# Moving the decayed-key products of a gated-recurrence mixer from GpSimd to VectorE

## The chip, the core and the metric

The kernel is one program on one NeuronCore of a Trainium2 chip. The core has five engines that run their own instruction streams and meet only at semaphores: TensorE (PE, matrix products and transposes; its weight loads are a row of their own, PEld), VectorE (DVE), ScalarE (ACT), GpSimd (POOL) and SyncE (SP, which here only issues DMAs). The metric is the device time of one execution in microseconds; the shown time is a median of several.

## What is computed

One inference step of a one-layer hybrid encoder over 1024 prompt rows and 32 sample rows of width 1024: a modulated norm, one input projection to 4096 columns, a retention mixer with 4 heads and an HGRN2 mixer with 4 heads, an output projection, a two-level mixture of experts, a last norm. The change touches the HGRN2 part:

```python
def hgrn2_chunk(S, q, k, v, logf):
    b = jnp.cumsum(logf, axis=1)
    inter = jnp.einsum('blhk,bhkv->blhv', q * jnp.exp(b), S)
    diff = b[:, :, None] - b[:, None, :]
    dec = jnp.exp(jnp.where(causal[None, :, :, None, None], diff, -jnp.inf))
    A = jnp.einsum('blhk,bmhk,blmhk->bhlm', q, k, dec)
    intra = jnp.einsum('bhlm,bmhv->blhv', A, v)
    k_dec = k * jnp.exp(bl[:, None] - b)          # bl is b at the chunk's last frame
    S_new = jnp.exp(bl)[..., None] * S + jnp.einsum('blhk,blhv->bhkv', k_dec, v)
```

Each head's output is then divided by its root mean square, scaled and gated.

## The kernel before

The program has five phases, one after the other: condition, mixers, output, experts, combine. Only `phase_mixers` is touched. It runs a hardware loop of 4 rounds, one pair of heads (one retention, one HGRN2) a round. A round first makes 12 transposed pieces of the projection on PE (`turned_piece`, lines 703 to 705), and then goes through 9 tiles of rows: tiles 0 to 7 of 128 rows, and tile 8, the sample's 32 rows. The tile loop is software-pipelined over 11 turns by hand: in turn i an engine works on tile i (projection, queries, keys, rotary), on tile i-1 (scores, masks, state products) and on tile i-2 (norm, output). Each engine's order is the order in which this code issues it; nothing else reorders it.

For one tile of the HGRN2 head these steps matter:

- `differences(i)`, DVE lines 885 to 894: a scan makes the running sum of the log decays in plane 8 of the tile `decay`, then plane 0 (distance to the tile's end) and planes 1 to 7 (distances to the middle of blocks of seven sizes, the levels).
- `decays(i)`, ACT lines 567 and 571: absolute value and exponential of all nine planes, in place; then `exp_done`.
- `queries(i)`, DVE lines 902 to 906: `last_f`, `q_in` = plane 8 times the queries (128 elements a partition), `q_lv` = planes 1 to 7 times the queries (896 elements).
- `keys(i)`, POOL line 495: `k_lv` = planes 0 to 7 times the keys `hk` (1024 elements); then `kl_done`.
- `rotary(i)`, DVE lines 987 to 994: rotates the retention head's query and key out of `qkv` and ends with `rot_done`.
- `values(i)`, ACT lines 641 and 644: copies `qkv` out of PSUM, waits for `rot_done`, makes the retention head's decayed key `k_dec`.
- `squares_of`, ACT lines 595 to 604: sums of squares of tile i-2 and a first estimate of its inverse root. `refine`, POOL lines 507 to 514: one Newton step on 128 x 2 numbers. `normalise`, ACT line 612: applies it.
- `copies`, ACT line 621: copies the three transposed tiles of tile i-1 out of PSUM (`turned`), which opens `scored(i-1)` on DVE, lines 964 to 977, then `gated`, lines 949 and 954.
- On PE: half a projection of tile i (12 matmuls, lines 729 to 731), in turns 1 to 8 eight small matmuls of the modulation (line 812), `scores(i-1)` (lines 744 to 766; it waits for `rot_done`, `kl_done`, `ql_done`), `turn_out(i-2)` (line 824; it waits for `normalise`), `retention_scores(i-1)` (line 775), the other half of the projection, `mix(i-1)` (lines 791 to 803).

ACT's order within a turn is fixed as: `squares_of(i-2)`, `normalise(i-2)`, `copies(i-1)`, `decays(i)`, `wide_levels(i-1)`, `values(i)`. DVE's is: `state(i-2)`, `differences(i)`, `scored(i-1)`, `gated(i-2)`, `queries(i)`, `rotary(i)`. POOL's is: `refine(i-2)`, `keys(i)`.

## Time and profile before

| | us |
|---|---|
| median of 3 runs | 1462.02 (1461.01 to 1463.92) |
| the profiled execution's own time | 1462.52 |
| its span, first to last instruction | 1460.9 |
| PE busy in the span | 1201.8 (82%) |
| DVE busy | 866.7 (59%) |
| ACT busy | 638.0 (44%) |
| POOL busy | 216.6 (15%) |
| POOL line 495 (`k_lv`), 40 instructions | 79.1 |

A busy share is an average over phases with different limits, so it does not say what bounds the mixers; the rows further down are read for that. "Idle before" and the name behind the arrow tell how long an engine had stood still before an instruction and which instruction ended the wait.

### The profile page before, as it was taken

Reading aid. Unit: us, or ns where it says so; the run is one execution under the profiler, and the core shown is the slowest. Engines: PE = TensorE matmul, PEld = TensorE weight load, DVE = VectorE, ACT = ScalarE, POOL = GpSimd, SP = SyncE. Lnnn points to the kernel's source line nnn. Section 1 sums busy time; section 2 is a strip of 40 time slices with the busy share of each in tenths; the row PEclk is TensorE's granted clock in tenths of the full one; section 3 lists DMA queues with packets and bytes.
Section 4 is the critical chain, followed back from the end, with each engine's and each line's share of the span. In section 5 each row is a group of like instructions: output and inputs, shape, how many; then the busy total and the mean of one; then the engine's idle time right before and its main releaser. Section 6 shows DMA issues by size and latency. Waiting matters only on the chain. (4 is left out here: it accounts for less than half of the span.)

```text
span 1460.9 us, 25004 instructions
## 1 busy us (share of the span) xinstructions
PE 1201.8 (82%) x7899; PEld 971.0 (66%) x7900; DVE 866.7 (59%) x1812; ACT 638.0 (44%) x1250; POOL 216.6 (15%) x307
## 2 busy tenths in 40 slices
PE   6479998999899989999489972989899999899900
PEld 1178776977597768877368751777677777777800
DVE  2614883368526872488545666677755575557339
ACT  3333554444434453345422213466544465446224
POOL 0200220022102220122000113011111101011132
PEclk9779999999999999999699985999899999999965
DMA  7512212221222122320453315979966696766155
GB/s 281 166 44 80 63 55 64 74 64 55 62 67 73 55 59 60 88 80 16 161 142 117 120 52 185 336 259 322 318 222 213 216 327 198 278 230 230 58 193 209
DMA packets 201385, 215.29 MB, mean 147 GB/s; under 512 B 15368, under 2 KB 166464, under 8 KB 201024
## 3 DMA queue, kind: packets, MB, share of 16 engines
q1 hardware_dynamic: 179136, 174.40, 37.6%
q0 software_dynamic: 10064, 34.42, 6.4%
q10 hardware_dynamic: 12112, 5.41, 1.3%
q8 instruction: 56, 0.92, 0.3%
q14 instruction: 17, 0.14, 0.0%
HBM read 187.40 MB, written 26.79 MB: 147 GB/s over the span
## 5 line engine op out<-in xcount | busy, mean ns | idle before, releaser
L703 PE MATMUL mixers_ps_proj<-early_h_hi,mixers_w_hi 128*128 128x352 f32 x384 | 127.7, 333 | 32.6 <-POOL mixers_a_hg L482 27.6
L1740 PE MATMUL experts_ps_g<-experts_w_hi,experts_x_hi 128*128 128x512 f32 x384 | 150.5, 392 | 2.2 <-DVE experts_x_lo L1669 2.2
L1742 PE MATMUL experts_ps_g<-experts_w_hi,experts_x_lo 128*128 128x512 f32 x384 | 150.2, 391 | 0.0
L1741 PE MATMUL experts_ps_g<-experts_w_lo,experts_x_hi 128*128 128x512 f32 x384 | 150.2, 391 | 0.0
L1664 DVE TENSOR_TENSOR experts_w_lo<-all_raw,experts_w_hi 128x1024 fp32r<-128x1024 f32 x96 | 113.9, 1223 | 28.3 <-ACT experts_w_hi L1613 25.2
L495 POOL TENSOR_TENSOR mixers_k_lv<-mixers_decay,mixers_hk 128x1024 f32<-128x1024 f32 (+2 forms) x40 | 79.1, 1981 | 334.4 <-ACT mixers_decay L571 334.4
L729 PE MATMUL mixers_ps_proj<-mixers_w_hi,early_h_hi 128*128 128x512 f32 (+1 forms) x288 | 119.1, 413 | 9.9 <-DVE mixers_w_lo L856 9.9
L704 PE MATMUL mixers_ps_proj<-early_h_lo,mixers_w_hi 128*128 128x352 f32 x384 | 125.8, 328 | 0.0
L705 PE MATMUL mixers_ps_proj<-early_h_hi,mixers_w_lo 128*128 128x352 f32 x384 | 125.8, 328 | 0.0
L1664 DVE TENSOR_TENSOR experts_w_lo<-experts_raw_more,experts_w_hi 128x1024 fp32r<-128x1024 f32 x96 | 111.8, 1222 | 14.5 <-ACT experts_w_hi L1613 13.1
L731 PE MATMUL mixers_ps_proj<-mixers_w_hi,early_h_lo 128*128 128x512 f32 (+1 forms) x288 | 113.7, 395 | 0.0
L730 PE MATMUL mixers_ps_proj<-mixers_w_lo,early_h_hi 128*128 128x512 f32 (+1 forms) x288 | 113.4, 394 | 0.0
L1613 ACT ACTIVATE experts_w_hi<-all_raw 128x1024 fp32r<-128x1024 f32 x96 | 97.7, 1055 | 13.6 <-PE experts_ps_g L1742 11.0
L856 DVE TENSOR_TENSOR mixers_w_lo<-all_raw,mixers_w_hi 128x1024 fp32r<-128x1024 f32 x32 | 43.3, 1366 | 93.7 <-ACT mixers_w_hi L529 93.7
L703 PEld LDWEIGHTS mixers_ps_proj<-early_h_hi,mixers_w_hi 128*128 128x128 f32 x384 | 74.5, 194 | 34.4 <-POOL mixers_a_hg L482 27.8
L1613 ACT ACTIVATE experts_w_hi<-experts_raw_more 128x1024 fp32r<-128x1024 f32 x96 | 94.4, 1059 | 0.0
L1740 PEld LDWEIGHTS experts_ps_g<-experts_w_hi,experts_x_hi 128*128 128x128 f32 x384 | 72.6, 189 | 17.6 <-issue 2.6
L1741 PEld LDWEIGHTS experts_ps_g<-experts_w_lo,experts_x_hi 128*128 128x128 f32 x384 | 72.7, 189 | 15.1
L1742 PEld LDWEIGHTS experts_ps_g<-experts_w_hi,experts_x_lo 128*128 128x128 f32 x384 | 72.6, 189 | 15.2
L1764 PE MATMUL experts_ps_y<-experts_w_hi,experts_h_hi 128*128 128x512 f32 x192 | 80.8, 421 | 0.3
L1765 PE MATMUL experts_ps_y<-experts_w_lo,experts_h_hi 128*128 128x512 f32 x192 | 78.0, 406 | 0.0
L1274 PE MATMUL output_ps_o<-output_w_hi,output_o_hi 128*128 128x512 f32 (+1 forms) x144 | 61.7, 428 | 19.8 <-DVE output_o_lo L1304 19.8
(269 smaller groups left out, 2613.9 us busy)
## 6 DMA issues: line engine op xcount, KB each, us to landing
experts_raw_more<-in_W_down_e_dram SPq DMA_DIRECT2D x128, 256.0 KB
all_raw<-in_W_gate_e_dram SPq DMA_DIRECT2D x96, 256.0 KB, 5.9
all_raw<-in_W_up_e_dram SPq DMA_DIRECT2D x96, 256.0 KB, 6.6
all_raw<-in_W_in_dram SPq DMA_DIRECT2D x32, 512.0 KB, 4.2
all_raw<-in_W_ada_dram SPq DMA_DIRECT2D x32, 512.0 KB, 3.9
y_scratch<-experts_y POOLq DMA_DIRECT2D x24, 512.0 KB
condition_w_ada_in<-in_W_ada_dram SPq DMA_DIRECT2D x4, 2048.0 KB, 8.1
experts_raw_more<-in_W_gate_e_dram SPq DMA_DIRECT2D x32, 256.0 KB
```

The source lines that it names most:

```text
L703: pe.matmul(out, whi, xhi, start=(k == 0), stop=False)
L704: pe.matmul(out, whi, xlo, start=False, stop=False)
L705: last = pe.matmul(out, wlo, xhi, start=False, stop=(k == KD - 1))
L729: pe.matmul(out, xhi, whi, start=(k == 0), stop=False)
L730: pe.matmul(out, xhi, wlo, start=False, stop=False)
L731: last = pe.matmul(out, xlo, whi, start=False, stop=(k == KD - 1))
L1613: act.activation(w_hi[:, c], raw[c], ACT.Copy).then_inc(hi_done, 1)
L1664: dve.tensor_tensor(w_lo[:, c], raw[c], f32(w_hi[:, c]), ALU.subtract).then_inc(lo_done, 1)
L1740: pe.matmul(out, x_hi[:, k, :], w_hi[:, c, at], start=(k == 0), stop=False)
L1741: pe.matmul(out, x_hi[:, k, :], w_lo[:, c, at], start=False, stop=False)
L1742: ins = pe.matmul(out, x_lo[:, k, :], w_hi[:, c, at], start=False, stop=(k == KD - 1))
L1764: pe.matmul(ps_y[m][:, :], h_hi[:, f, :], w_hi[:, 8 + f, at], start=(f == 0), stop=False)
```

## The change

The function `keys` leaves POOL's program and goes, with the same operands, into DVE's, between `queries(i)` and `rotary(i)`. Its waits for `exp_done` and `lv_done` are dropped there, because `queries(i)` has just waited for both on the same engine; the wait for `hk_done` in tile 0 stays. `refine` stays on POOL.

```diff
@@ -483,19 +483,6 @@
-                def keys(i):
-
-                    w = width(i)
-                    pool.wait_ge(exp_done, n[9] + (i + 1))
-                    pool.wait_ge(lv_done, n[9] + i)
-                    if i == 0:
-                        pool.wait_ge(hk_done, n[1] + 1)
-                    kb = hk[:, i * P:i * P + w]
-                    for c, (lo, hi) in enumerate([(0, 8)] if w == P else [(0, 1), (3, 8)]):
-                        last = pool.tensor_tensor(k_lv[:, lo:hi, 0:w], decay[:, lo:hi, 0:w],
-                                                  kb.unsqueeze(1).broadcast_to([P, hi - lo, w]), ALU.mult)
-                    last.then_inc(kl_done, 1)
@@ -516,8 +503,6 @@
                 for i in range(NT + 2):
                     if i >= 2:
                         refine(i - 2)
-                    if i < NT:
-                        keys(i)
@@ -907,6 +892,17 @@
+                def keys(i):
+
+                    w = width(i)
+                    if i == 0:
+                        dve.wait_ge(hk_done, n[1] + 1)
+                    kb = hk[:, i * P:i * P + w]
+                    for c, (lo, hi) in enumerate([(0, 8)] if w == P else [(0, 1), (3, 8)]):
+                        last = dve.tensor_tensor(k_lv[:, lo:hi, 0:w], decay[:, lo:hi, 0:w],
+                                                 kb.unsqueeze(1).broadcast_to([P, hi - lo, w]), ALU.mult)
+                    last.then_inc(kl_done, 1)
@@ -1005,6 +1001,7 @@
                     if i < NT:
                         queries(i)
+                        keys(i)
                         rotary(i)
```

DVE in turn 1, before, from the masks of tile 0 to the rotary step of tile 1:

```order
L973 TENSOR_REDUCE mixers_a_hg<-mixers_masked 32x32 x4
L977 ISA
L977 TENSOR_TENSOR mixers_a_ret<-mixers_ps_a,early_tables 128x128
L902 COPY mixers_last_f<-mixers_decay 128x1
L905 TENSOR_TENSOR mixers_q_in<-mixers_decay,mixers_hq 128x128
L906 TENSOR_TENSOR mixers_q_lv<-mixers_decay,mixers_hq 128x896
L987 TENSOR_TENSOR mixers_qk_cos<-mixers_qkv,early_tables 128x256
```

The same place after the change (later lines have moved up, by 15 before the new function and by 4 behind it):

```order
L969 TENSOR_REDUCE mixers_a_hg<-mixers_masked 32x32 x4
L973 ISA
L973 TENSOR_TENSOR mixers_a_ret<-mixers_ps_a,early_tables 128x128
L887 COPY mixers_last_f<-mixers_decay 128x1
L890 TENSOR_TENSOR mixers_q_in<-mixers_decay,mixers_hq 128x128
L891 TENSOR_TENSOR mixers_q_lv<-mixers_decay,mixers_hq 128x896
L902 TENSOR_TENSOR mixers_k_lv<-mixers_decay,mixers_hk 128x1024
L983 TENSOR_TENSOR mixers_qk_cos<-mixers_qkv,early_tables 128x256
```

One instruction of 1024 elements a partition now stands between `q_lv` and the rotary step; nothing else on DVE moved.

DVE in turn 8, where the tile has 32 columns, after the change:

```order
L890 TENSOR_TENSOR mixers_q_in<-mixers_decay,mixers_hq 128x32
L891 TENSOR_TENSOR mixers_q_lv<-mixers_decay,mixers_hq 128x5x32
L902 TENSOR_TENSOR mixers_k_lv<-mixers_decay,mixers_hk 128x32
L902 TENSOR_TENSOR mixers_k_lv<-mixers_decay,mixers_hk 128x5x32
L983 TENSOR_TENSOR mixers_qk_cos<-mixers_qkv,early_tables 32x256
```

Here two instructions stand in the new place.

POOL in one of the turns 2 to 7, before, the keys of one tile and then the refinement of an older one:

```order
L489 REGISTER_ALU
L495 TENSOR_TENSOR mixers_k_lv<-mixers_decay,mixers_hk 128x1024
L507 TENSOR_TENSOR mixers_norm<-mixers_norm 128x2
L508 REGISTER_ALU
L509 TENSOR_TENSOR mixers_norm<-mixers_norm,mixers_mean_sq 128x2
L510 REGISTER_ALU
L512 TENSOR_SCALAR mixers_norm<-mixers_norm 128x2
L513 REGISTER_ALU
L514 TENSOR_TENSOR mixers_norm<-mixers_norm 128x2
```

and after:

```order
L493 REGISTER_ALU
L494 TENSOR_TENSOR mixers_norm<-mixers_norm 128x2
L495 REGISTER_ALU
L496 TENSOR_TENSOR mixers_norm<-mixers_norm,mixers_mean_sq 128x2
L497 REGISTER_ALU
L499 TENSOR_SCALAR mixers_norm<-mixers_norm 128x2
L500 REGISTER_ALU
L501 TENSOR_TENSOR mixers_norm<-mixers_norm 128x2
```

POOL is left with the four small instructions of the refinement. PE, ACT and SP issue what they issued before.

## Rows read from the trace of the kernel before

**Rows 1.** The page's busy line; then who PE waited for, whole span.

```profile
PE 1201.8 (82%) x7899; PEld 971.0 (66%) x7900; DVE 866.7 (59%) x1812; ACT 638.0 (44%) x1250; POOL 216.6 (15%) x307
...
PE mixers_ps_ot L824 <- ACT mixers_normed L612: 28.4, 32, 2.8
```

**Rows 2.** Windows, round 2's tiles: length, PE, PEld, DVE, ACT, POOL, clock, DMA, GB/s.

```profile
448.00:557.00 109.00, 100.18 (x987) 75.86 (x988) 78.21 (x235) 50.79 (x153) 24.75 (x45) 0.97 0.22 64
```

**Rows 3.** Timeline of PE, round 2, turn 7 (start, duration, idle before).

```profile
527.24 0.41 PE L824 MATMUL mixers_ps_ot<-all_consts_sb,mixers_normed 128*128 128x128 f32 x2 [0.53 <-ACT mixers_normed L612]
```

**Rows 4.** Timeline of DVE, round 2, turn 6 and the start of turn 7.

```profile
516.23 0.29 DVE L964 TENSOR_TENSOR mixers_qd_t<-mixers_turned,early_tables 128x128 f32<-128x128 f32 x1 [1.66 <-ACT mixers_turned L621]
...
519.89 1.17 DVE L905 TENSOR_TENSOR mixers_q_in<-mixers_decay,mixers_hq 128x128 f32<-128x128 f32 x1
520.98 1.08 DVE L906 TENSOR_TENSOR mixers_q_lv<-mixers_decay,mixers_hq 128x896 f32<-128x896 f32 x1
521.98 0.41 DVE L987 TENSOR_TENSOR mixers_qk_cos<-mixers_qkv,early_tables 128x256 f32<-128x256 f32 x1
...
522.97 0.29 DVE L994 TENSOR_TENSOR mixers_rot<-mixers_qk_cos,mixers_qk_sin 128x128 f32<-128x128 f32 x1
...
527.51 0.29 DVE L964 TENSOR_TENSOR mixers_qd_t<-mixers_turned,early_tables 128x128 f32<-128x128 f32 x1 [1.66 <-ACT mixers_turned L621]
```

**Rows 5.** Timeline of ACT, the same stretch.

```profile
523.29 0.40 ACT L644 ACTIVATE mixers_k_dec<-mixers_rot,mixers_kd_col 128x128 f32<-128x128 f32 x1 [3.14 <-DVE mixers_rot L994]
...
523.85 0.28 ACT L595 ACTIVATE mixers_squares<-mixers_ps_o 128x128 f32<-128x128 f32 x1 [0.15 <-issue]
...
526.47 0.63 ACT L612 ACTIVATE mixers_normed<-mixers_ps_o,mixers_norm 128x128 f32<-128x128 f32 x2 [1.24 <-POOL mixers_norm L514]
526.99 0.49 ACT L621 ACTIVATE mixers_turned<-mixers_ps_tr 128x384 f32<-128x384 f32 x1
```

**Rows 6.** Timeline of POOL, the same stretch.

```profile
518.53 2.37 POOL L495 TENSOR_TENSOR mixers_k_lv<-mixers_decay,mixers_hk 128x1024 f32<-128x1024 f32 x1 [3.38 <-ACT mixers_decay L571]
525.30 0.19 POOL L507 TENSOR_TENSOR mixers_norm<-mixers_norm 128x2 f32<-128x2 f32 x1 [4.40 <-ACT mixers_mean_sq L604]
...
526.24 0.20 POOL L514 TENSOR_TENSOR mixers_norm<-mixers_norm 128x2 f32<-128x2 f32 x1
```

**Rows 7.** Timeline of DVE, round 2, end of the pieces and turn 0.

```profile
446.72 1.23 DVE L856 TENSOR_TENSOR mixers_w_lo<-all_raw,mixers_w_hi 128x1024 fp32r<-128x1024 f32 x1 [0.42 <-ACT mixers_w_hi L529]
...
447.92 0.28 DVE L905 TENSOR_TENSOR mixers_q_in<-mixers_decay,mixers_hq 128x128 f32<-128x128 f32 x1
448.12 1.08 DVE L906 TENSOR_TENSOR mixers_q_lv<-mixers_decay,mixers_hq 128x896 f32<-128x896 f32 x1
454.57 0.43 DVE L987 TENSOR_TENSOR mixers_qk_cos<-mixers_qkv,early_tables 128x256 f32<-128x256 f32 x1 [5.36 <-ACT mixers_qkv L641]
```

**Rows 8.** DVE groups by shape, 97 to 700 us (busy, mean ns).

```profile
L905 DVE TENSOR_TENSOR mixers_q_in<-mixers_decay,mixers_hq 128x128 f32<-128x128 f32 x32 | 36.0, 1125 | 0.0
```

**Rows 9.** Timeline of DVE, round 2, turn 1.

```profile
462.64 1.74 DVE L905 TENSOR_TENSOR mixers_q_in<-mixers_decay,mixers_hq 128x128 f32<-128x128 f32 x1
464.31 1.08 DVE L906 TENSOR_TENSOR mixers_q_lv<-mixers_decay,mixers_hq 128x896 f32<-128x896 f32 x1
```

**Rows 10.** Timeline of DVE, round 2, turn 8.

```profile
542.43 0.17 DVE L905 TENSOR_TENSOR mixers_q_in<-mixers_decay,mixers_hq 128x32 f32<-128x32 f32 x1
542.53 0.31 DVE L906 TENSOR_TENSOR mixers_q_lv<-mixers_decay,mixers_hq 128x160 f32<-128x160 f32 x1
542.77 0.41 DVE L987 TENSOR_TENSOR mixers_qk_cos<-mixers_qkv,early_tables 32x256 f32<-32x256 f32 x1
```

**Rows 11.** Timeline of PE, round 2, turn 9, scores of tile 8.

```profile
544.17 0.28 PE L744 MATMUL mixers_ps_tr<-all_consts_sb,mixers_rot 32*128 32x32 f32 x2 [0.71 <-DVE mixers_rot L994]
```

**Rows 12.** Timeline of POOL, round 2, turn 4, first step of a refinement.

```profile
491.28 0.38 POOL L507 TENSOR_TENSOR mixers_norm<-mixers_norm 128x2 f32<-128x2 f32 x1 [4.41 <-ACT mixers_mean_sq L604]
```

**Rows 13.** Windows, round 2, turn 9, columns as in rows 2.

```profile
549.00:553.00 4.00, 3.46 (x13) 1.74 (x13) 2.04 (x6) 0.05 (x1) 0.00 (x0) 0.50 0.30 82
```

## The prediction

> **What bounds the kernel now.** The page gives PE as the busiest engine by far, 1201.8 of 1460.9 us, DVE 866.7, POOL 216.6 [rows 1]. In the stretch of round 2 that holds the tile turns PE is busy 100.2 of 109 us and DVE 78.2 [rows 2]. By shares the change looks harmless or good: the engine with the most room to wait gives work to one that has 31 us free. The next view says otherwise. The list of PE's waits shows one that comes back in each turn: the transposes of `turn_out` (line 824) wait for ACT's normalised tile (line 612), 32 times, 28.4 us in all [rows 1]; in a middle turn it is 0.53 us [rows 3]. So in each turn something other than PE ends last, and the third view, the timelines of one turn on DVE, ACT and POOL, is read backwards from there. Start to start:
>
> DVE 516.23 (masks, `scored`) to 519.89 (`q_in`), 3.66; to 520.98 (`q_lv`), 1.09; to 521.98 (rotary), 1.00; to 522.97 (its last step), 0.99 [rows 4]. ACT's `k_dec` starts 0.32 later, at 523.29, after 3.14 us of waiting for just that step; its squares at 523.85 (0.56) [rows 5]. POOL's refinement starts at 525.30 (1.45) and its last step at 526.24 (0.94) [rows 6]. ACT normalises at 526.47 (0.23) and copies `turned` at 526.99 (0.52) [rows 5]. DVE's next `scored` starts at 527.51 (0.52), after 1.66 us of waiting for that copy [rows 4]. The sum is 11.28 us, and that is the turn's length (527.51 less 516.23). This is a closed ring: **DVE's stretch from `scored` to rotary lies in it**, since ACT cannot begin the squares before `k_dec`, which waits for rotary. PE's work of a turn is 0.53 us shorter than the ring. Whatever is added to DVE between the masks and the last step of rotary lengthens each turn in full.
>
> POOL's key product is not in the ring: it starts at 518.53, runs 2.37 and ends at 520.90 [rows 6], and PE asks for it only behind rotary and the half projection. But it costs the ring something all the same. `q_in` has 128 elements and takes 0.28 us in turn 0, where POOL is idle [rows 7], and 1.17 in turn 6 [rows 4]: it starts at 519.89 and is done at 521.06, just behind POOL's end at 520.90. In turn 1 it takes 1.74 [rows 9]. I read it as blocked until POOL has finished.
>
> The Trainium skill says the same: in "SBUF — State Buffer", section "SBUF: two separate sides", VectorE and GpSimd share one port pair as an exclusive lock, held for a whole instruction, when VectorE reads two SBUF inputs. By that rule the excess of `q_in` must vanish with the key product; the trace agrees (0.28 against 1.17). The figures for it in the sum are those of the rows.
>
> **The change, part by part.**
>
> *Taken off DVE: the blocked time of `q_in`.* Its 32 wide instances hold 36.0 us [rows 8]. Four are turn 0 at 0.28 [rows 7] and four are turn 1 at 1.74 [rows 9]; that leaves 27.9 us for the 24 of turns 2 to 7, 1.163 each. The next instruction starts 0.08 before the end (1.17 long, 1.09 to the next start) [rows 4]. So it occupies 1.083 of the ring, and 0.20 once free (447.92 to 448.12) [rows 7]: **0.883 saved** in each of 24 turns. In turn 1 it is 464.31 less 462.64, 1.67 [rows 9], so 1.47 is saved there, 4 times.
>
> *Put on DVE: the key product.* No row shows it on DVE. The nearest is `q_lv`, the same operation and types over 896 elements: 1.08 us, 1.00 to the next start [rows 4]. 128 elements take 0.28, so 768 more take 0.80, or 1.04 ns each, and 1024 elements take 1.08 + 0.13 = 1.21. A two-input subtraction of 1024 elements takes 1.23 [rows 7]. Less the overlap of 0.08 this is **1.14 added** to the ring. Bounds: 1.00 (as `q_lv`) and 1.23 (no overlap).
>
> *Turns 2 to 7:* 1.14 - 0.883 = +0.257; 24 of them give **+6.2 us**. The saving is smaller than the price because the blocked time was only the tail of POOL's 2.37 us; its first 1.36 (518.53 to 519.89) lay beside DVE's masks and output products.
>
> *Turn 1:* 1.14 - 1.47 = -0.33, four times, **-1.3 us**. PE's 32 waits at line 824 are eight a round, and the first of the eight stands behind turn 1 [rows 1], so PE follows.
>
> *Turn 8:* the 32-column tile. `q_in` takes 0.17, so it was not blocked; the two new instructions cost 0.10 (as `q_in`'s 542.43 to 542.53) and 0.24 (as `q_lv`'s 542.53 to 542.77) [rows 10]. PE waits for this rotary directly, 0.71 us [rows 11], and nothing covers it: 4 x 0.34 = **+1.4 us**.
>
> *Turn 0:* the key product lands behind `q_lv` (448.12), ahead of 5.36 us in which DVE waits for the first projection [rows 7]: nothing; without that cover it would be 1.14, four times. Its absence from POOL frees the second last weight split on DVE, but the last one, at 446.72, waits for ACT anyway (0.42 idle) [rows 7]: nothing.
>
> *Who now gets its keys later.* Before they were there at 520.90; after at about 519.89 + 0.20 + 1.00 + 1.21 = 522.30. PE's scores want them together with the last step of rotary, which starts at 522.97 [rows 4] and will start later, so no new wait. `differences` waits for `kl_done`, now its own engine's and long given. POOL loses its wait for the exponentials, and the refinement stands first in its queue; it was started by ACT's squares before, with POOL 4.40 us idle [rows 6], so this gives nothing.
>
> *A term with no fixed sign.* The first step of the refinement takes 0.19 us [rows 6] or 0.38 [rows 12], in the same place, beside DVE's `differences`. It is in the ring. Of the 24 in turns 3 to 8, 7 are longer than 0.19 and 17 are not, and a shift of some 0.01 us in the start seems to decide. After the change all could be short, 7 x -0.19 = -1.3 us, or all long, 17 x 0.19 = +3.2. I take no change.
>
> Sum: 6.2 - 1.3 + 1.4 = **+6.2 us** (rounded only here). Phases before and behind the mixers hold none of these steps and start one after the other, so the span goes from 1460.9 to 1467.1, the profiled run from 1462.5 to 1468.7, and the median, 0.5 below it, to **1468.2 us**.
>
> **Rivals.**
>
> *The turn is not held by the ring (no change).* If ACT or POOL had slack that I do not see, for instance if the squares could start on something other than `k_dec`, the 0.257 would be absorbed, and with it turn 1's gain; only turn 8 would stay: 0 to +1.4, so 1462.0 to 1463.4. For it: DVE has 1.66 us free in a turn. Against it: that idle time is a wait for the ring's own last link, and the ring's links sum to the turn without a remainder. Chance 0.08. The key product priced at 1.00 with all refinements short (+6.2 less 28 x 0.14 less 1.3, about +1.0) also ends here: 0.04.
>
> *POOL's key product was the slow thing (faster).* If the scores or the squares did wait for the keys in some way that the releasers hide, giving them to the engine that makes them in 1.21 instead of 2.37 would shorten turns 1 to 7 by up to 1.16 less the 0.257 that DVE adds, 28 x 0.9 = 25 us: 1437. It decides if the keys are the last of the scores' inputs; the rows have them ready 2.1 us ahead of rotary's last step (520.90 against 522.97) [rows 4, 6]. Half of such an effect would do for a visible gain. Chance 0.05. The Trainium skill supports the move as such: "GPSIMD Engine Reference", section "Engine selection", puts elementwise products of two inputs on VectorE because GpSimd is about half as fast. The trace shows that ratio (2.37 against an estimated 1.21), but the rule compares durations and says nothing of what lies beside other work.
>
> *`q_in` is not blocked by POOL (much slower).* If its 1.17 us came from something else in that place, such as reading the exponentials just written, nothing would be saved: 28 x 1.14 + 1.4 = +33, so 1495. It decides if `q_in` stays above 1 us. Against it: 0.28 in turn 0 and 0.17 in turn 8, and the end that follows POOL's in turn 6. Chance 0.03.
>
> *TensorE loses its clock more often (slower).* The granted clock is 0.97 over the turns [rows 2], and it falls to 0.50, the 1.2 GHz level, in turn 9, where PE has stood still for longer [rows 13]. If the longer waits brought such a stretch of 4 us at half speed or more into turns 1 to 8 of a round, PE would lose some 2 us or more each time: +8 or more on top, about 1476. Against it: PE waited 28.4/32 = 0.89 us a turn on average at that clock [rows 1], and would now wait some 0.2 more. Chance 0.03.
>
> *All refinements long:* +9.4, 1471.4. Chance 0.04.
>
> **How the numbers follow.** The forecast has the rest, 0.73. Slower by over 0.2% (2.9 us, about what a measurement of this kernel can tell from no change): 0.73 + 0.03 + 0.03 + 0.04 = 0.83. Within: 0.12. Faster: 0.05. The ends: the key product at 1.00 instead of 1.14 takes 3.9 us off, which with short refinements gives 1463.0; at 1.23 it adds 2.5, with long ones 1473.9. Both terms at their ends at once is unlikely, so the range takes the middle of them and the edge of the next cases: 1464.3 to 1472.2.
>
> **What would show it.** `q_in` at 0.28 in all wide turns; the key product on DVE at 1.21, the next start 1.14 behind it; turns of 11.53 us in place of 11.28, turn 1 shorter by 0.33; PE's wait at line 824 up from 0.53 to about 0.8; POOL with only its four small steps; POOL's 79 us of key products gone and DVE busier by some 10 us in all (32 x 1.21 and 4 x 0.48 on, 27 us of blocked `q_in` and some of the weight splits off). The forecast is wrong if turns keep 11.28 (the ring is not what I think), if `q_in` stays long, or if the clock in turns 1 to 8 falls below what it was.

## The result, and the profile after

| | before | changed |
|---|---|---|
| median, beside each other on one chip | 1461.51 (4 runs, 1460.63 to 1463.92) | 1470.97 (4 runs, 1470.53 to 1478.55) |
| ratio, with its 95% interval | | 1.0079 [1.0052, 1.0106] |
| profiled execution; its span | 1462.52; 1460.9 | 1478.55; 1476.7 |

The changed kernel is slower, by 7.6 to 15.5 us. The forecast was slower by 6.2 (a ratio of 1.0042): the sign is right, the size too small. Two further runs of the changed kernel took 1474.59 and 1475.13. A repeat of the pair gave 1.011 [1.0079, 1.014]. So the profile has to answer two questions: are the steps of the forecast there at their sizes, and where is the rest?

The page of the changed kernel (busy line) and the list of PE's waits, which answer [rows 1]:

```profile
PE 1208.2 (82%) x7899; PEld 975.7 (66%) x7900; DVE 872.2 (59%) x1852; ACT 637.6 (43%) x1250; POOL 138.5 (9%) x267
...
PE mixers_ps_ot L809 <- ACT mixers_normed L597: 32.8, 32, 2.9
...
PE mixers_ps_proj L688 <- ACT mixers_hk L540: 5.1, 3, 1.9
PE mixers_ps_tr L729 <- DVE mixers_rot L990: 4.2, 4, 1.0
```

POOL loses 78.1 us. PE's wait for the normalised tile grows by 4.4 us in all. The wait for `hk` is new: before, PE never waited for it. The wait for rotary's last step, in turn 9 of each round, was 2.8 us in all before and is 4.2 now.

Timeline of DVE, changed kernel, round 2, turn 6, which answers [rows 4]:

```profile
525.67 0.29 DVE L960 TENSOR_TENSOR mixers_qd_t<-mixers_turned,early_tables 128x128 f32<-128x128 f32 x1 [1.66 <-ACT mixers_turned L606]
...
529.33 0.27 DVE L890 TENSOR_TENSOR mixers_q_in<-mixers_decay,mixers_hq 128x128 f32<-128x128 f32 x1
529.53 1.07 DVE L891 TENSOR_TENSOR mixers_q_lv<-mixers_decay,mixers_hq 128x896 f32<-128x896 f32 x1
530.53 1.21 DVE L902 TENSOR_TENSOR mixers_k_lv<-mixers_decay,mixers_hk 128x1024 f32<-128x1024 f32 x1
531.67 0.41 DVE L983 TENSOR_TENSOR mixers_qk_cos<-mixers_qkv,early_tables 128x256 f32<-128x256 f32 x1
...
532.65 0.28 DVE L990 TENSOR_TENSOR mixers_rot<-mixers_qk_cos,mixers_qk_sin 128x128 f32<-128x128 f32 x1
...
537.19 0.29 DVE L960 TENSOR_TENSOR mixers_qd_t<-mixers_turned,early_tables 128x128 f32<-128x128 f32 x1 [1.66 <-ACT mixers_turned L606]
```

ACT, POOL and PE in the same turn, one after the other, which answer [rows 5], [rows 6] and [rows 3]:

```profile
532.97 0.40 ACT L629 ACTIVATE mixers_k_dec<-mixers_rot,mixers_kd_col 128x128 f32<-128x128 f32 x1 [3.35 <-DVE mixers_rot L990]
533.53 0.28 ACT L580 ACTIVATE mixers_squares<-mixers_ps_o 128x128 f32<-128x128 f32 x1 [0.16 <-issue]
...
536.15 0.63 ACT L597 ACTIVATE mixers_normed<-mixers_ps_o,mixers_norm 128x128 f32<-128x128 f32 x2 [1.25 <-POOL mixers_norm L501]
536.67 0.49 ACT L606 ACTIVATE mixers_turned<-mixers_ps_tr 128x384 f32<-128x384 f32 x1
```

```profile
534.98 0.20 POOL L494 TENSOR_TENSOR mixers_norm<-mixers_norm 128x2 f32<-128x2 f32 x1 [10.38 <-ACT mixers_mean_sq L589]
```

```profile
536.92 0.30 PE L809 MATMUL mixers_ps_ot<-all_consts_sb,mixers_normed 128*128 128x128 f32 x1 [0.76 <-ACT mixers_normed L597]
```

Read the ring again, start to start: 3.66 to `q_in`, 0.20, 1.00, 1.14 (the key product), 0.98 to rotary's last step, 0.32 to `k_dec`, 0.56, 1.45, 1.17, 0.52, 0.52. The sum is 11.52 us, against 11.28 before, and no link but the two edited ones moved by more than 0.01. The same view of turn 1 and the DVE groups by shape (97 to 715 us) answer [rows 8, 9]:

```profile
471.44 0.28 DVE L890 TENSOR_TENSOR mixers_q_in<-mixers_decay,mixers_hq 128x128 f32<-128x128 f32 x1
...
482.85 0.27 DVE L890 TENSOR_TENSOR mixers_q_in<-mixers_decay,mixers_hq 128x128 f32<-128x128 f32 x1
```

```profile
L902 DVE TENSOR_TENSOR mixers_k_lv<-mixers_decay,mixers_hk 128x1024 f32<-128x1024 f32 x32 | 38.7, 1208 | 0.0
...
L890 DVE TENSOR_TENSOR mixers_q_in<-mixers_decay,mixers_hq 128x128 f32<-128x128 f32 x32 | 8.7, 272 | 0.0
```

So the forecast's steps are there. For the rest the trace is cut at marks that both kernels have: the start of `q_in` in turns 0, 1 and 8 ("t0", "t1", "t8") and PE's `turn_out` of tiles 7 and 8 ("ot7", "ot8"), worked out from the timelines. Sums over the rounds:

```
us                                     before   changed   difference
start to the first projection piece     82.60     83.81      +1.2
first piece to t0 of round 0            50.94     51.29      +0.4
t0 to t1, 4 rounds                      58.91     60.24      +1.3
t1 to t8, 4 rounds                     319.09    323.33      +4.2
t8 to ot7, 4 rounds                     22.26     23.64      +1.4
ot7 to ot8, 4 rounds                    39.08     42.22      +3.1
ot8 to t0 of the next round, 3         140.08    142.31      +2.2
ot8 of round 3 to the output phase      10.84     11.42      +0.6
mixers: first piece to output phase    641.2     654.5      +13.3
```

The forecast's parts are the lines "t1 to t8" and "t8 to ot7": +5.6. Another 7.6 us of the mixers lies at the ends and starts of the rounds, where the change adds nothing. The remaining 2.5 us of the span lie outside the mixers, where executions of identical code also differ (from its first to its last product on PE, the experts' phase took 485.9 us before, 488.1 changed, and 478 to 502 in the traces of the kernels below, none of which touches it). The gap repeats in a second pair of traces, 639.9 and 653.2 us for the mixers; there the forecast's two lines give +6.6 and the rest +6.7.

What happens at a round's end shows in the windows (length, PE, PEld, DVE, ACT, POOL, granted clock, DMA, GB/s). Before, round 2's end, the stretches behind [rows 13]:

```profile
553.00:557.00 4.00, 4.00 (x18) 4.00 (x19) 0.61 (x2) 2.72 (x10) 0.73 (x4) 0.67 0.39 115
557.00:561.00 4.00, 2.41 (x16) 2.09 (x15) 1.62 (x4) 0.13 (x1) 0.00 (x0) 1.00 0.14 32
```

The changed kernel, the same place:

```profile
557.00:561.00 4.00, 2.11 (x9) 0.94 (x9) 2.57 (x8) 1.82 (x5) 0.37 (x2) 0.56 0.00 0
561.00:565.00 4.00, 4.00 (x14) 3.01 (x15) 0.90 (x3) 1.29 (x7) 0.21 (x2) 0.50 0.68 196
565.00:569.00 4.00, 4.00 (x19) 4.00 (x18) 0.00 (x0) 1.55 (x3) 0.53 (x3) 0.66 0.02 4
```

The clock is at its 1.2 GHz level (0.50) for 10.24 us at the end of rounds 0 to 2, where it was 6.82 before (548.80 to 555.62; now 557.48 to 567.72), and returns closer to the end of the next round's first piece. PE has no wait in that piece, so until the clock returns each matmul in it costs 0.29 us instead of 0.16. PE, before and then changed, around the point where the clock returns:

```profile
555.42 0.42 PE L705 MATMUL mixers_ps_proj<-early_h_hi,mixers_w_lo 128*128 128x352 f32 x1
555.68 0.32 PE L703 MATMUL mixers_ps_proj<-early_h_hi,mixers_w_hi 128*128 128x352 f32 x1
...
558.18 0.31 PE L824 MATMUL mixers_ps_ot<-all_consts_sb,mixers_normed 32*128 32x32 f32 x2
```

```profile
567.44 0.46 PE L690 MATMUL mixers_ps_proj<-early_h_hi,mixers_w_lo 128*128 128x352 f32 x1
567.74 0.32 PE L688 MATMUL mixers_ps_proj<-early_h_hi,mixers_w_hi 128*128 128x352 f32 x1
...
569.27 0.31 PE L809 MATMUL mixers_ps_ot<-all_consts_sb,mixers_normed 32*128 32x32 f32 x2
```

Before, 2.50 us of the piece ran at full speed ahead of `turn_out`; now 1.53.

The length of a low stretch by itself does not set the cost; where it ends does. Before, it ended 7.62 us behind ot7 in this round, and ot7 to ot8 took 10.18 us; in the changed kernel it ended 9.46 behind ot7, and the stretch took 11.01. In rounds 0 and 1 of the changed kernel the end lies 10.38 and 10.57 behind ot7, for 11.43 and 11.51 us. The same line runs through rounds 0 to 2 of all 14 traces of this study without a fill in turn 9 (12 kernels): 42 points, with 0.46 us more from ot7 to ot8 for each us that the low stretch ends later, and none more than 0.06 us off the line. From the matmuls one expects about that: in 1 us at 0.29 us each PE does 0.55 us of the work at 0.16.

A second thing follows on ACT's queue, which issues the store of the sample's state. Before, then changed, then PE in the changed kernel:

```profile
559.67 0.42 ACTq L651 DMA_DIRECT2D ut_state_ret_sample_dram<-mixers_s_sample  x1
...
561.51 1.28 ACT L554 ACT_TABLE_LOAD   x1 [4.38 <-issue]
```

```profile
570.76 1.72 ACTq L636 DMA_DIRECT2D ut_state_ret_sample_dram<-mixers_s_sample  x1
...
573.90 1.28 ACT L539 ACT_TABLE_LOAD   x1 [6.51 <-issue]
```

```profile
576.07 0.43 PE L688 MATMUL mixers_ps_proj<-early_h_hi,mixers_w_hi 128*128 128x352 f32 x1 [1.72 <-ACT mixers_hk L540]
```

The issue takes 0.42 us in every round before and 1.33, 1.05 and 1.72 in rounds 0 to 2 now. The sigmoids of the new round stand behind it on ACT and start later, and PE waits for `hk`: 3 times, 5.1 us. Its waits called "issue" at the same line shrank from 4.9 to 1.3, so 1.5 us of this is a net loss. Third, turn 0 of round 2 has a low stretch of its own that the kernel before has in no round. Windows over its start, before and then changed:

```profile
448.00:452.00 4.00, 3.93 (x17) 3.21 (x18) 1.21 (x3) 0.00 (x0) 0.00 (x0) 1.00 0.84 240
```

```profile
455.00:459.00 4.00, 3.51 (x9) 2.85 (x10) 2.76 (x5) 0.00 (x0) 0.00 (x0) 0.57 0.69 204
```

It begins (455.08) in PE's wait of 2.5 us for the last weight split, which both kernels have in every round, and turn 0 takes 16.09 us instead of 14.72.

### The profile page after: what moved, and what is told of

Read it like the earlier page. It is cut to its first block and busy times, and to the rows that moved or that the text cites. A ratio compares the mean times of both kernels' runs of the same rounds, so it can differ in the third digit from the quotient of the medians.

```text
span 1476.7 us, 24964 instructions
## 1 busy us (share of the span) xinstructions
PE 1208.2 (82%) x7899; PEld 975.7 (66%) x7900; DVE 872.2 (59%) x1852; ACT 637.6 (43%) x1250; POOL 138.5 (9%) x267
## 5 line engine op out<-in xcount | busy, mean ns | idle before, releaser
L841 DVE TENSOR_TENSOR mixers_w_lo<-all_raw,mixers_w_hi 128x1024 fp32r<-128x1024 f32 x32 | 38.6, 1221 | 98.5 <-ACT mixers_w_hi L514 98.5
L1720 PE MATMUL experts_ps_x<-all_consts_sb,experts_x_rows 128*128 128x128 f32 x200 | 32.4, 314 | 59.1 <-DMA experts_x_rows<-h_scratch,experts_index 59.1
```

## The experiments

Theory: the ring sets turns 1 to 7, and the surplus at the rounds' ends is a second cost. The rival for the first part is that the moved product hurts in some other way (contention on DVE, its effect on PE's scores). For the second part one theory is that the surplus comes from the product itself or from tile 8's small instructions, through PE's longer standstill in turns 8 and 9. The other is that any shift of a round's end can bring it (called the place theory).

**The pair again.** No edits: `a_again` is the changed kernel, `b_again` the one before.

> The changed kernel once more, unchanged, for a second trace and a tighter ratio. Ring theory (what the prediction rests on): turns 2 to 7 are 11.53 us in place of 11.28, in all some +6 us, so about 1468. Clock theory (a second cost beside the ring): TensorE's granted clock stays at 0.50 longer at the end of each round, 10.2 us against 6.8 in the profiled execution, and the sum is +9 to +12, about 1471 to 1474, with executions some us apart according to where the low stretches fall. A trace with 6.8 us at the end of the rounds and a time near 1468 would say that the profiled execution was an outlier.

> The kernel before once more, for a second trace. Clock theory: the low stretches at the end of the rounds have the same length in the three rounds, since the round's length (157.0 us) repeats; they may be 6.8 or 10.2 us. If they are 6.8 here too, the longer ones belong to the change and not to chance.

Measured: 1479.55 (1476.83 to 1480.98) beside 1462.47 (1453.36 to 1471.21), ratio 1.011; `b_again` 1462.27 in one run. The changed kernel came out above what either theory had asked for, while `b_again` agrees with the first run of before. The mixers take 653.2 and 639.9 us. In the changed kernel the low stretches at the ends are 10.24 us long again, the one in turn 0 of round 2 is there again, and long issues (0.84 to 1.21 us) are in it alone. `b_again` did not do as expected in one respect: its low stretches are 6.8, 6.8 and 10.2 us long, not of one length. The long one began 1.97 us ahead of ot7 and ended 8.27 behind it, and ot7 to ot8 took 10.47 us, not 11. Two traces of each kernel agree, so the extra cost belongs to the kernel, not to one execution.

**The ring.** `keys_last` puts the key product behind rotary, out of the ring:

```diff
                         queries(i)
-                        keys(i)
                         rotary(i)
+                        keys(i)
```

> Keys on VectorE as in the change, but behind the rotary step. Ring theory: q_in is free of GpSimd (-0.88 a turn) and the key product lies outside the ring, so the ring is 10.40 us and TensorE's own work of 10.75 takes over: turns of about 10.75 to 10.8, TensorE's wait for the normalised tile gone or under 0.1 us in turns 2 to 8; 24 to 28 turns x 0.5 = 12 to 14 us faster than before, about 1449. If the ring is not what sets the turn, it stays at 1462 or above.

Measured: 1450.68 (7 runs), ratio 0.9908 [0.987, 0.9946]. Turns of 10.78 us in the middle of a round, 10.70 in the mean of turns 1 to 7. Two of PE's waits:

```profile
PE mixers_ps_ot L809 <- ACT mixers_normed L597: 9.6, 4, 2.4
PE mixers_ps_tr L729 <- DVE mixers_k_lv L902: 4.7, 4, 1.2
```

Four waits for the normalised tile are left of 32, those of turn 9. The same instruction on the same engine, some 1.2 us later in the order, costs nothing in turns 2 to 8. In turn 9 the scores now wait for the small tile's key products, 4.7 us in all, where they waited 2.8 for rotary before and 4.2 in the change, but the wait for the normalised tile is shorter there: t8 to ot7 is 5.67 to 5.70 us, 5.57 before and 5.91 in the change. So its place in the ring was the price, not its being on DVE. The ring by itself would be 1.14 shorter, 10.38, below what the turns take; what holds them at 10.78 is not shown in full, since the two rotary kernels below issue the same work on PE in turns of 10.50.

**The blocked `q_in`.** `pool_twin` is the changed kernel with a product of the same size and types added on GpSimd at the old place, on constants, into a tile of its own that nothing reads (the lines that work; the rest of the edit makes the tile and the semaphore):

```diff
+                    pool.wait_ge(exp_done, n[9] + (i + 1))
+                    pool.wait_ge(twin_done, n[8] + i)
+                    pool.tensor_tensor(spare[:, :, :], s.tables[:, 0:1024].rearrange("p (c n) -> p c n", c=8),
+                                       s.consts[:, 0:P].unsqueeze(1).broadcast_to([P, 8, P]), ALU.mult).then_inc(twin_done, 1)
```

> The change, with a product of the same size added on GpSimd at the time of its old key product, from constants into a tile that nothing reads. Port theory (q_in was blocked by GpSimd's instruction): q_in is back at 1.15 to 1.17 us in turns 2 to 7, the key product on VectorE behind it stays at 1.21, and turns are 11.53 + 0.88 = 12.41 us. If q_in was slow for another reason, it stays at 0.28 and turns stay at 11.53.

Measured: 1500.39 (one run). From turn 4 on, `turn_out` follows `turn_out` in 12.51 to 12.53 us, 1.00 above the change where 0.88 was expected; `q_in` takes 1.25 to 1.34 us in turns 2 to 7, a little more than the 1.15 to 1.18 of before. DVE and POOL in one turn:

```profile
535.26 1.27 DVE L901 TENSOR_TENSOR mixers_q_in<-mixers_decay,mixers_hq 128x128 f32<-128x128 f32 x1
536.46 1.08 DVE L902 TENSOR_TENSOR mixers_q_lv<-mixers_decay,mixers_hq 128x896 f32<-128x896 f32 x1
```

```profile
533.98 2.41 POOL L492 TENSOR_TENSOR mixers_spare<-early_tables,all_consts_sb 128x1024 f32<-128x1024 f32 x1 [3.45 <-ACT mixers_decay L567]
```

POOL ends at 536.39, `q_in` at 536.53. The operands are other tiles, so no dependence joins the two; `q_in` is held by GpSimd's being at work. The Trainium skill ("SBUF — State Buffer", "SBUF: two separate sides") calls this an exclusive lock of a port pair held for a whole instruction; by that rule it must return with any such product, and it did.

The same trace answers the prediction's rival on the clock. PE's wait for the normalised tile has grown to 1.75 to 1.99 us in turns 2 to 8, and two low stretches of 3.41 us fall into the tile turns of each round, where the kernel before and the changed one have none. They do not lengthen the turn, which the ring sets: PE's next wait behind each of the eight is 0.26 to 0.41 us, and the turns stay at 12.5.

**Tile 8's share.** `tile8_pool` gives only the 32-column tile's keys back to GpSimd (with the function that makes them there, not shown):

```diff
                     if i >= 2:
                         refine(i - 2)
+                    if i == NP_T:
+                        keys(i)
...
-                        keys(i)
+                        if i < NP_T:
+                            keys(i)
```

> The change with the keys of the 32-row tile left on GpSimd. Ring theory: the 0.34 us of turn 8 go, 4 times, so 1.4 us less than the change. Clock theory, form a (the longer standstill of TensorE in turns 8 and 9 prolongs the low stretch): the low stretches return to 6.8 us and the kernel is 4 to 6 us faster than the change. Form b (only the place of the round in the clock's own course counts): no such gain beyond 1.4.

Measured: 1474.09 (12 runs, 1459.26 to 1484.59), ratio 1.0053 [1.0022, 1.0084], beside 1479.55 for the change. By the time alone form a would do (5.5 us less); the trace, of the longest of the twelve executions, says otherwise. The stretch from t8 to ot7 is back to 5.57 in all rounds, so its 1.4 us are tile 8's. The surplus at the ends stays in rounds 0 and 2 (low stretches of 10.24, 11.48 and 11.49 us from ot7 to ot8) and is gone in round 1 (6.82, issue of 0.42, 46.33 to the next t0), while turn 0 of round 3 has a low stretch and takes 16.15: the mixers take 649.6. With the work of turn 8 as it was, two rounds of three still have the surplus; it comes and goes round by round.

**Filling turn 9.** `b_fill`, `a_fill` and `keys_fill` add 22 unused matmuls to PE in turn 9 of the kernel before, the changed one and `keys_last`, to hide the low stretch there:

```diff
+                    if i == NT:
+                        pe.wait_ge(v_done, n[9] + 8)
+                        fill(FILL)
...
+                    if i == NT:
+                        fill(FILL2)
```

> The same fill in the kernel before. Clock theory: the low stretches of 6.8 us go here too, with 1 to 2 us a round to gain, so about 1457 to 1460; and the change with the fill less this one is the ring alone, +5.6 to +6.2 us. If the difference between the filled kernels stays at +11 or more, the clock at the end of the rounds does not explain the miss.

> The change with 22 extra matmuls of 352 columns in turn 9 of each round, into a PSUM bank that nothing reads (17 ahead of the transposes that wait 2.85 us for the normalised tile, 5 ahead of the products that wait for the masks), so that TensorE hardly stands still there. Clock theory: the low stretches of 10.2 us at the end of rounds 0 to 2 go or fall to 3.4 to 6.8, the pieces that follow run at full clock, and the kernel gains 4 to 8 us on the change in spite of the added work, to about 1468. If the clock is not the second cost, the fill gains nothing or costs up to 1 us a round.

> Keys behind the rotary step, with the same fill. Ring theory: turns of 10.70 us as in the run without the fill (79.78 less 4.86 us from turn 1 to turn 8). Clock theory: the three low stretches of 10.2 us shrink and the kernel is 3 to 8 us faster than without the fill, about 1444. Without that theory: the same as without the fill or up to 3 us slower.

Measured: ratios 0.9977 [0.9942, 1.0012], 1.0072 [1.0031, 1.0114] and 0.9878 [0.9819, 0.9937]; medians 1464.14, 1476.62 and 1447.88; mixers 643.1, 653.1 and 627.9. None of the three gains that the clock theory had forecast came in full. The low stretch did not go. It moved behind ot8, into the pieces of the next round (246.68 to 253.50 in `a_fill`, where ot8 is at 244.27), and what ot7 to ot8 gained, ot8 to t0 gave back. The medians of the filled pair differ by 12.5 us, over the 11 at which the expectation had given the clock up, and their mixers by 10.0, between the ring's 5.6 and the unfilled 13.3. Since the fill did not remove the low stretch, the test settles nothing. It shows only that a stretch driven out of one place turned up in the next.

**A delay with nothing of the change in it.** The kernel before, with 3, 8, 15 or 21 extra matmuls (0.16 us each) ahead of one projection piece in each round, results unused; `a_delay13` has 13 of them in the changed kernel:

```diff
+                for k in range(EXTRA if (j, c) == (1, 1) else 0):
+                    pe.matmul(ps_p[(3 * j + c) % 2][:, 0:PIECE], w_hi[:, k % KD, j, :], s.h_hi[:, k % KD, at],
+                              start=True, stop=True)
```

> The kernel before with 3 extra matmuls in front of one piece of each round, 0.48 us a round, 1.9 us in all. Read from the trace, from the first piece to the output phase (641.2 and 639.9 us in the two traces of before). Place theory: the kernel before lies at an edge, so that even this brings 10.2 us low stretches or a slow round start in some rounds: 645 to 652. Theory that the second cost needs longer standstills: 642 to 643.

> The kernel before with 8 extra matmuls of 352 columns in front of one piece of each round (0.16 us each at full clock, results overwritten): 1.28 us more a round, about what the ring costs in the change, but far from the tile turns. Place theory (the low stretch at the end of a round falls where the round's end happens to lie, and the kernel before lies well): the low stretches grow to 10.2 us here too, rounds are about 160 us from turn 0 to turn 0 instead of 157.0, and the kernel is 10 to 12 us slower. Theory that only longer standstills of TensorE in turns 8 and 9 prolong the low stretch: it stays at 6.8, rounds are 158.3, and the kernel is 4 x 1.28 = 5 us slower.

> The same with 15, 2.40 us a round, 9.6 in all. Place theory: rounds near 160.4 again whatever is added between 1.3 and 3.4 us: 654 to 658, as with 8 (654.6) and with 21 (657.9). Other theory: the added work and nothing else, 650 to 651.

> The same with 21 extra matmuls, 3.36 us a round. Place theory: the end of the round is moved by about as much as two neighbouring possible starts of a low stretch lie apart in the trace (6.8 and 10.2 us long stretches differ by 3.4), so it lies as well as in the kernel before: low stretches of 6.8 us, rounds of 160.4 us, 13 to 14 us slower. It would then hardly be slower than the one with 8. Other theory: 13 to 14 us as well, but the one with 8 at only 5.

> The change with 13 extra matmuls at the same place, 2.08 us a round. Place theory: its round without the longer low stretch would be 157.0 + 1.35 = 158.4 us, with the delay 160.4, which lies well again: low stretches of 6.8 us, rounds of 160.4 where the change has 160.0 to 160.2 without the delay. So 8.3 us of added work cost between -1 and +3 us against the change. Other theory: the full 8.3 us, low stretches still 10.2.

Measured (medians beside their own runs of before; mixers from the traces):

```
             added us,   time and ratio                     mixers   over     beyond the
             4 rounds                                       us       base     added work
b_delay3      1.9        1469.79 (one run)                  650.6    +9.4     +7.5
b_delay8      5.1        1471.57, 1.0101 [1.0043, 1.0159]   654.6    +13.4    +8.3
b_delay15     9.6        1468.13 (one run)                  654.6    +13.4    +3.8
b_delay21    13.4        1477.70, 1.0136 [1.0082, 1.019]    657.9    +16.7    +3.3
the change    5.6 (ring) 1470.97, 1.0079 [1.0052, 1.0106]   654.5    +13.3    +7.7
a_delay13     8.3        1488.82, 1.0195 [1.0146, 1.0245]   666.9    +12.4    +4.1 (over the changed kernel)
```

`b_delay8` adds 1.28 us a round to the kernel before, about what the change adds (1.4), and pays a surplus of the same size. By the times too it is slower than its 5.1 us of work: by 6.3 us at the lower end of its interval. The surplus is made of the same things, but in other shares:

```
beyond the added work, us   turn 0   ot7 to ot8   ot8 to the next t0
the change                   1.3        3.1              2.2
b_delay3                     4.7        0.6              2.3
b_delay8                     6.0        0.7              1.8
```

Its window over the start of turn 0 in round 2, which was at 1.00 before, and ACT's queue at the end of that round:

```profile
453.00:457.00 4.00, 2.32 (x7) 1.82 (x8) 2.49 (x4) 0.64 (x2) 0.00 (x0) 0.77 0.57 159
```

```profile
568.63 2.02 ACTq L652 DMA_DIRECT2D t_state_hgrn_sample_dram<-mixers_s_sample  x1
```

Even 0.48 us a round (`b_delay3`) brings a low stretch into turn 0 of rounds 1 to 3 (t0 to t1 of 16.27 to 16.30 for 14.73) and issues of 2.16 and 1.38 us. Turn 0 is long (16.0 us or more) in each of the 20 rounds of the study with a low stretch at its start, and in no other. So the costs of turn 0 and of the issues need nothing of keys, DVE or GpSimd: in these traces the kernel before lies in a favourable place, and small delays lose it. The largest part of the change's surplus, 3.1 us from ot7 to ot8, no delay of the kernel before brought back: its low stretches ended 7.5 to 8.9 us behind ot7. It is not the keys' alone either, since round 1 of `b_rotary_first` below, with the keys on GpSimd, has a low stretch that ends 10.31 behind ot7 and 11.41 us from ot7 to ot8. Why the changed kernel ends late there in all three rounds stays open.

Two cautions. `b_delay3` and `b_delay15` are one run each, and their times (1469.79 and 1468.13) are no more than 1.8 us from the 1468.02 of the kernel before beside them, whose seven runs spread over 18 us; only the traces show the loss. And the base of the mixers, 641.2, is the first trace of the kernel before (639.9 in the second); none was taken beside the delays, so a difference between these executions and those is not ruled out.

The place theory failed where it was made precise. It had `b_delay21` (6.8 us at the ends, 13 to 14 us in all: it paid 16.7, with 10.24 at one end and a low stretch in turn 0 of round 3) and `a_delay13` back in a place without surplus, and `a_delay13` has low stretches of 10.24 us at three ends and one in turn 0 of each round. Nor did any delay tried come back to no surplus. What exactly decides where a low stretch begins stays open.

**Taking more out of the ring.** `b_rotary_first` is the kernel before (keys on GpSimd) with one line moved; `rotary_first` is the changed kernel with the order rotary, queries, keys:

```diff
-                        queries(i)
                         rotary(i)
+                        queries(i)
```

> The kernel before, keys still on GpSimd, with the rotary step ahead of queries on VectorE. Port theory: now the rotary step's first product (two inputs in SBUF) is the one that is held until GpSimd's product ends, about 1.1 us longer than its 0.41, and q_in falls to 0.28. Ring theory: q_in and q_lv leave the ring (-2.09), the held time stays in it (+1.0 or so), the ring is about 10.2 us, below TensorE's 10.70, so turns are 10.70 us as with the keys behind the rotary step, and the stretch from turn 1 to turn 8 is 74.9 us against 79.8. The time is 10 to 15 us below the kernel before, according to where the ends of the rounds fall, so about 1450. If the gain of that other version came from taking the keys off GpSimd, turns stay near 11.3 here.

> Keys on VectorE as in the change, but rotary step first, then queries, then keys. Ring theory: queries and keys are both out of the ring, nothing is held by GpSimd; VectorE's work of a turn (about 7.8 us with the keys, by the rows) is still below TensorE's, so turns are 10.50 us as with rotary first and the keys on GpSimd, and the time is the same as that kernel's within 0.4%, near 1436. If keys on VectorE cost more than they give even outside the ring, turns are longer than 10.50 and the time is above 1440.

Measured: `b_rotary_first` 1435.51 (1428.48 to 1446.8), ratio 0.9817 [0.9743, 0.9891]; `rotary_first` 1446.04, ratio 0.9857 [0.9795, 0.9919]. Turns of 10.50 us in both; mixers 618.2 and 622.6 us. A turn of `b_rotary_first` on DVE, and its line in the list of PE's waits:

```profile
501.69 0.29 DVE L964 TENSOR_TENSOR mixers_qd_t<-mixers_turned,early_tables 128x128 f32<-128x128 f32 x1 [0.81 <-ACT mixers_turned L621]
...
505.86 0.78 DVE L987 TENSOR_TENSOR mixers_qk_cos<-mixers_qkv,early_tables 128x256 f32<-128x256 f32 x1 [0.48 <-ACT mixers_qkv L641]
...
507.49 0.28 DVE L905 TENSOR_TENSOR mixers_q_in<-mixers_decay,mixers_hq 128x128 f32<-128x128 f32 x1
...
512.19 0.29 DVE L964 TENSOR_TENSOR mixers_qd_t<-mixers_turned,early_tables 128x128 f32<-128x128 f32 x1 [0.82 <-ACT mixers_turned L621]
```

```profile
PE mixers_ps_ot L824 <- ACT mixers_normed L612: 11.4, 4, 2.8
```

Rotary now waits for `qkv`, which waits for PE, and PE no longer waits for the normalised tile in turns 2 to 8. The queries, 1.20 us of them, left the ring. The blocking moved to the first rotary product (0.77 to 0.98 us in turns 1 to 7 for 0.41), where it costs 0.37 in a middle turn instead of 0.88. The expectation had the turns at 10.70, the first rotary product 1.1 us longer and the time near 1450; all three came out smaller. `rotary_first` has the turns that it was given, but its time is above the 1440 that was named as the sign of a cost of the keys outside the ring. The traces show a part of it: from t0 to t8 it takes 82.8 us a round, `b_rotary_first` 82.2. Beyond that the intervals of the two ratios overlap, so the times do not tell the two kernels apart. `b_rotary_first` has the lowest median of the study, 1.8% ahead of before.

## Why the prediction was too low, point by point

- *The closed ring.* Right. Its links sum to 11.52 and the turns are 11.49 to 11.54 from turn 4 on, or 11.71 to 11.73 where the refinement's first step is the long one. `keys_last` and the two rotary kernels show that what stands outside it costs next to nothing. One side remark was off: PE's work of a turn is not 0.53 us below the old ring of 11.28 but at least 0.78, since the rotary kernels have turns of 10.50.
- *`q_in` freed, 0.883 a turn.* Right: 0.27 to 0.28 in all wide turns, 36.0 us before and 8.7 now. `pool_twin` shows the cause.
- *The key product, 1.21 long and 1.14 to the next start.* Right: 1.208 mean, 1.14. Turns 2 to 7 grew by 0.24 to 0.25 where like refinements are compared (forecast 0.257), turn 1 shrank from 11.74 to 11.41 (forecast -0.33), turn 8 cost 0.34 to 0.35. Sum forecast +6.2, measured +5.6, and +6.6 in the second pair of traces.
- *The refinement's long step, no change.* Right within its bounds, but it moved by itself: of the 24 steps counted, 7 were long before and 6 after, and a long one in turn 2 (0.48 us) was gone, some 0.4 us together. In the second pair it went the other way, 6 long and 10. This is the difference between +5.6 and +6.6.
- *PE's wait 0.53 to about 0.8.* Right, 0.76. *DVE busier by 10 us.* Too high, 5.5: durations were added (40.6 on, 27.3 and 4.7 off, so 8.6), but the page counts the 0.08 us shared by neighbours once, 2.6 us over 32 products. That leaves 6.0.
- *What failed: the sum ended at the tiles.* It took the same time for everything outside the turns that it had priced: "Phases before and behind the mixers hold none of these steps", and turn 0 and the rounds' ends got nothing. The same mixers paid 7.6 us there: 3.1 from ot7 to ot8 in rounds 0 to 2, 2.2 from ot8 to t0, 1.3 in turn 0 of round 2, 1.0 at the two outer ends. The rival on the clock named the mechanism, but looked for it "into turns 1 to 8" and gave it 0.03; in those turns the clock held. [Rows 13] had shown the low stretch beside the first piece, which PE runs without a wait, and that should have made the round's end a term with bounds. The trace of before held a bound: of the 24 matmuls of the first piece, 9 were at 0.29 us already, and the other 15, at 0.16, could each cost 0.13 more, up to 2.0 us a round, three times. Measured were 0.8 to 1.2 us a round.
- *The range.* Its upper end, 1472.2, came from the key product's price and the refinements alone. The median of 1470.97 lies inside it, but that is luck, since the room up to there was kept for terms that did not move. The ratio says more: on the 1462.02 us from which the forecast started it gives 1473.6, and the repeat's 1478.1, both outside. With a term for the rounds' ends of 0 to 9 us the range would have held them.

What is shown: where the 7.6 us were paid, that ot7 to ot8 follows the end of the low stretch, and that a delay alone brings a surplus of this size in turn 0 and behind ot8 (`b_delay3`, `b_delay8`). Three things stay open: what sets the beginning and the end of a low stretch, why in the changed kernel it ends late behind ot7 in all three rounds, and why the issue of the state's store takes 0.42 us in some rounds and 1 to 2 in others. The long issues come only in kernels whose round end was shifted, though not in all their rounds, and no run here separates the cause.

## What to carry to other kernels

Before work is moved from a slow engine to a fast one, find the closed chain that sets the turn, and ask whether the old place was outside it and the new one is inside. Here the product on GpSimd took twice as long and cost only 0.88 us of 2.37, while moving rotary ahead of the queries, with no work moved to another engine, gave 1.8%. And where a loop holds stretches at a lower granted clock, a shift of half a microsecond may change what runs inside them (one trace, `b_delay3`; with 1.28 us also the times): give the loop's ends a term and bounds in the sum.

## What the runs showed of the hardware

- GpSimd's product of 2.37 us held a VectorE product of two SBUF tiles that started beside it until it ended: `q_in` 0.28 to 1.17 (1.27 with the added product), the first rotary product 0.41 to 0.78, the second last weight split of a round 1.23 to 2.38 (mean of all 32 splits: 1.37 before, 1.22 changed). A product of the same size with one input in PSUM, `a_ret` at 518.91 in the middle of GpSimd's, took its usual 0.29.
- From the first turn 0 to the last turn 8, the stretches of the mixers at a granted clock of 0.50 were 3.4, 6.8 or 10.2 us long. Their cost followed from where they ended, 0.46 us per us behind ot7 (42 rounds in 14 traces). Filling PE's idle time in one place did not remove them but moved them.
- PE waits of 1.75 to 1.99 us in the tile turns came with low stretches in these turns (`pool_twin`); waits of up to 0.98 us did not (the changed kernel).
- Issuing one DMA of the same size from ACT's queue took 0.39 to 2.21 us, in the same place of the program.
- With a delay of 0.48 us a round the mixers took 9.4 us more over four rounds than in the trace of before (one trace).
